# One step of a two-layer hybrid decoder: the order of TensorE's work inside a unit of the prompt's attention

## The reference

```
s[q, k] = q.k / 8 + c[q] - c[k]      causal; c: running sum of log forget values
o       = softmax(s) . v
```

## Time and profile before

| | |
|---|---|
| median of 3 runs | 1531.43 us (1527.56 to 1536.17) |
| the profiled execution's own time | 1532.03 us |
| its span | 1530.2 us |
| mean granted TensorE clock | 0.961 of full speed |
| busy share of the span: TensorE, VectorE, ScalarE, GpSimd | 93%, 33%, 32%, 39% |
| the loop over the units | from about 899.4 to 1040.3 us of the span |

### The profile page before, as it was taken

The page is one execution under the profiler, slowest core; times in us unless marked ns, Lnnn a source line. Parts: engine busy times, 40 slices in busy tenths (PEclk is TensorE's granted clock), DMA queues, the critical chain, the costliest instruction groups (busy, mean ns, idle before and its releaser), DMA issues.

```text
span 1530.2 us, 30086 instructions
## 1 busy us (share of the span) xinstructions
PE 1416.5 (93%) x11701; PEld 1293.3 (85%) x11701; DVE 503.3 (33%) x719; ACT 482.1 (32%) x622; POOL 601.4 (39%) x295
## 2 busy tenths in 40 slices
PE   7999899799999999996999969997969999999995
PEld 5999858689999999995899934446969999999994
DVE  2353853720000000147311179796540000000035
ACT  2331212353433421224211232324354334331123
POOL 2333301565555554364323230000654554554351
PEclk9999978999999999998999979899989999999998
DMA  5222201213323232221689998670213233232211
GB/s 215 83 77 86 74 27 40 78 30 113 99 72 114 94 113 90 95 74 33 215 279 319 328 203 309 214 247 14 83 42 97 84 95 96 82 117 95 94 39 56
DMA packets 88020, 180.30 MB, mean 118 GB/s; under 512 B 30025, under 2 KB 30042, under 8 KB 87442
## 3 DMA queue, kind: packets, MB, share of 16 engines
q1 hardware_dynamic: 87202, 175.46, 35.3%
q0 software_dynamic: 752, 3.92, 1.2%
HBM read 173.29 MB, written 6.05 MB: 117 GB/s over the span
## 4 chain that ended last, share of the span: by engine, by line
PE 75%; DVE 12%; issue 5%; ACT 2%; SPq 2%; DMA 2%; POOL 1%; DVEq 0%; ACTq 0%; POOLq 0%
PE ps L837 63%; DVE x L1342 2%; DVE pj L1729 2%; DVE rstd L1317 1%; SPq L331 1%; PE ps L1190 1%; PE ps L1189 1%; POOL wl L698 1%; DVE x L1331 1%; PE ps L1024 1%; DVE rstd L1339 1%; PE ps L1141 1%; PE ps L956 1%; PE ps L1219 1%; DVE x L1308 1%
## 5 line engine op out<-in xcount | busy, mean ns | idle before, releaser
L698 POOL TENSOR_TENSOR wl<-raw,wh 128x1024 fp32r<-128x1024 f32 (+1 forms) x180 | 460.7, 2559 | 801.0 <-ACT wh L385 801.0
L837 PE MATMUL ps<-xh,wh 128*128 128x260 f32 x2368 | 487.4, 287 | 57.0 <-POOL xl L763 36.2
L837 PE MATMUL ps<-xh,wl 128*128 128x260 f32 x2368 | 479.8, 284 | 0.0
L837 PE MATMUL ps<-xl,wh 128*128 128x260 f32 x2368 | 479.5, 284 | 0.0
L385 ACT ACTIVATE wh<-raw 128x1024 fp32r<-128x1024 f32 (+1 forms) x180 | 201.1, 1117 | 762.7 <-PE ps L837 756.9
L837 PEld LDWEIGHTS ps<-xh,wh 128*128 128x128 f32 x2368 | 367.9, 190 | 72.5 <-issue 41.9
L837 PEld LDWEIGHTS ps<-xh,wl 128*128 128x128 f32 x2368 | 368.1, 190 | 0.0
L837 PEld LDWEIGHTS ps<-xl,wh 128*128 128x128 f32 x2368 | 367.6, 190 | 0.0
L1383 DVE TENSOR_TENSOR hid_t<-ps,gate_t 128x520 f32<-128x520 f32 x44 | 30.8, 700 | 476.7 <-PE ps L837 476.7
L837 PE MATMUL ps<-hh,wh 128*128 128x260 f32 x704 | 142.3, 283 | 0.0
L837 PE MATMUL ps<-hh,wl 128*128 128x260 f32 x704 | 141.6, 282 | 0.0
(11 more groups left out here) (277 smaller groups left out, 1139.5 us busy)
## 6 DMA issues: line engine op xcount, KB each, us to landing
raw<-in_w_f_in SPq DMA_DIRECT2D x88, 512.0 KB, 3.5
pages<-in_cache_kt SPq DMA_DIRECT2D x128, 256.0 KB, 4.2
pages<-in_cache_v SPq DMA_DIRECT2D x128, 256.0 KB, 4.2
raw<-in_w_f_out SPq DMA_DIRECT2D x32, 704.0 KB, 4.0
raw<-in_w_ab_in SPq DMA_DIRECT2D x24, 512.0 KB, 3.6
raw<-in_w_cd_in SPq DMA_DIRECT2D x20, 512.0 KB, 4.3
raw<-in_w_ab_out SPq DMA_DIRECT2D x8, 512.0 KB, 3.6
raw<-in_w_cd_out SPq DMA_DIRECT2D x8, 512.0 KB, 5.4
```

The source lines that it names most:

```text
L698: nc.gpsimd.tensor_tensor(wl[:, j % SPLIT, 0:b * P], raw[:, j, 0:b * P], wh[:, j % SPLIT, 0:b * P].bitcast(F32), ALU.subtract).then_inc(w_ ...
L837: mm = nc.tensor.matmul(out[h], w[:, slot, block_at * P:block_at * P + P], rows[:, k, HT * h:HT * h + HT], start=start and a, stop=stop and z)
```

## The change

In TensorE's loop the value slot of unit u is issued ahead of the scores of unit u + 1 instead of behind them. Nothing else is changed: the same instructions with the same waits, on all engines.

```diff
             with pe.Fori(0, 2) as i:
                 scores(i, 0)
                 for u in range(16):
+                    value_slot(i, u)
                     if u < 15:
                         scores(i, u + 1)
-                    value_slot(i, u)
                     turned(i, u)
                     if u > 0:
                         outputs(i, u - 1)
```

## The result

The changed kernel takes 1542.92 us in the median of 12 runs (1537.82 to 1547.58), the kernel before 1534.62 in the median of 12 (1527.56 to 1539.44). The ratio is 1.0055, with a 95% interval of 1.0036 to 1.0075: slower by some 8.4 us, 5.5 to 11.5. The forecast of +6.7 us lies in that interval and 1542.9 lies in the stated range, at its upper edge, but I held no change (within 0.5%) for the likeliest, and the ratio lies beyond that bound. By how much is not sharp: the interval reaches down to 0.36%; a second measurement of the same kernel, further down, gave 1.0064 (1.0039 to 1.0089). Two runs of kernels further down, far from all others of their kernel (2772.53 us of all_but_u0_first, and 1787.27 us of warm_u0_first), are left out of every number.

The account below looks back on a forecast made before the run. The prediction took a closed chain between VectorE and TensorE, every four units, to bound the kernel. Its terms, 8 x 0.99 - 1.2 = +6.7 us, gave a median of 1538.1 us, range 1533 to 1543.

Parts of the forecast that it names:

- The closed chain: Every four units of the loop: VectorE's half 7.83 us, then TensorE's half 8.00 us, together 15.83 us a group.
- not slower: Rival: in the steady groups VectorE alone sets the pace, later scores still come in time; 1530.2 us, chance 0.09.
- The 16 us more of VectorE's waits: Sign in the loop: VectorE's waits for scores would rise by about 16 us from 15.3.
- Its price: Value slot(2) ahead of scores(3) lengthens TensorE's half by 0.99 us, eight times per execution: 7.9 us.
- the new neighbours: Some five new seams a group on TensorE's half, 2 us less or more in all; taken as nothing.
- Value slot(1) "nothing": In TensorE's half, slot(1) ahead of scores(2) delays maximum(2), but TensorE is last by 0.15 us: costs nothing.
- Value slots(3) and (0): In VectorE's half, TensorE's work of 6.7 us fits in 7.83 in both orders: costs nothing.
- The pages, -1.2 us: At slot(4) of the first iteration, an earlier load lands 2.4 us earlier and removes 1.2 us of wait.
- My rival with late pages: Slot(4)'s load lands where it did: 1.5 us more than the forecast, 1539.6 us, chance 0.13.
- The first units and the turn, none moves: Iteration start and turn: scores(0), slot(0), scores(1) precede transposes(0) in either order, so no time changes.
- The clock rival: One more drop of TensorE's clock, most likely ending the second iteration: 4.7 us more, 1542.8 us, chance 0.14.
- Drops in every group: Rival: each group's new TensorE wait lowers the clock, eight drops at 4.7 us: 38 us, 1576, chance 0.02.

Follow-up runs that it names:

- all_but_u0_first: The changed kernel without its slot(0): every value slot with u > 0 ahead of the scores; 1.0071 to the kernel before.
- warm_u0_first: The kernel before plus unread filler products in TensorE's waits, and slot(0) of each iteration ahead of scores(1); 0.9984 to the kernel before.
- The two kernels with short taps: Kernel before and changed kernel, each with two of four taps cut from 512 to 8 columns; 0.9971 and 0.9976 to the kernel before.
- u0_late: The kernel before with slot(0) of each iteration behind transposes(0), ahead of scores(2); 1.0013 to the kernel before.
- warm_before: The kernel before, its order kept, plus products that nobody reads in TensorE's waits; 1.0016 to the kernel before.
- slots03_first: The kernel before with only the value slots of u % 4 = 0 and 3 ahead of the scores; 1.0034 to the kernel before.
- after_two_taps: The changed kernel with two of each unit's four taps cut from 512 to 8 columns; 0.9976 to the kernel before.

## Why the prediction was right or wrong

**The closed chain: right.** VectorE's half stayed at 7.83 us, TensorE's grew, in each of eight groups, and the waits ahead of transposes(3) became 0.93 us (1.23 in the first group) and 1.82 at the end of the iterations. The two kernels with short taps show that nothing else in the group costs. One sign that I had named was wrong: a maximum(3) that follows scaling(2) without a wait was to mean "not slower". It came, and the kernel is slower, because the slot had already held back maximum(2) and VectorE's own work from there led to maximum(3). The 16 us more of VectorE's waits could not have come out either: VectorE does the same work, so in a loop that I took to be 7.9 us longer its waits can't grow by twice that.

**Its price: 0.85 instead of 0.99.** Forecast 7.9 us for eight groups, measured 6.8 (0.85 or 0.86 in the five stretches that lie wholly at the upper clock, taken for all eight). TensorE's half held the slot's 0.99 us, but the new neighbours that I had put at nothing gave back 0.14: scores(2), now followed by transposes(1), took 1.65 us instead of 1.74 (959.37 to 961.02), and transposes(1) with outputs(0), now followed by a slot, 0.68 instead of 0.73 (961.02 to 961.70).

**Value slot(1) "nothing": wrong.** The step compared when TensorE and VectorE would be ready for maximum(3) with slot(2) moved as well, found them 0.15 us apart, and gave the whole price to slot(2). Slot(1) alone costs 0.74 us a group, slot(2) alone 1.00. Two paths of nearly equal length led to maximum(3), so either slot is enough: undoing slot(2) would have gained some 0.1 us a group, and undoing slot(1) nothing.

**Value slots(3) and (0): nearly right,** 0.13 us a group by themselves.

**The pages, -1.2 us: wrong.** I took the end of the bounds in which the load lands as much earlier as it starts. With the 480 KB issued at 900 to 902 and the loads behind it, they landed some 20 us behind the loop's start in either order, and with that transfer out of the way they took 3 to 4 us: it held them. My rival with late pages is what happened, once with a wait of 0.73 us (second profile) and once hidden by a start at the lower clock.

**"The first units and the turn, none moves", and with it a clock term of nothing: the step that failed.** Counted in instructions the step is true, scores(0), slot(0) and scores(1) come ahead of transposes(0) in either order. But these units run at the lower clock, and the sum took it that this lasts as long as before. The changed kernel's mean clock is 0.0033 lower (0.9572 and 0.9571 in 20 runs together, against 0.9605), and u0_first, which moves nothing but slot(0) in the two first units, is 1.0022 slower, 3.4 us, at a clock 0.0034 lower. The groups' 6.8 us are 0.44%, just inside the bound; measured are 0.55%. The terms do not add up exactly: 6.8 + 3.4 = 10.2 us, for 8.4 measured, which is inside its interval (5.5 to 11.5). The miss of the bound is small against the noise; what is clear of it is that the clock fell.

The clock rival was right that TensorE's clock would take a part, and wrong about the place: it was looked for at the end of the second iteration, where the stretch still shows 1.00. Drops in every group did not occur; the steady group shows 1.00 with waits of 0.93 us in it. The rule of the Trainium skill that I set beside it (TensorE: Matmul & The Clock Gate, "A second HAM failure mode: psum-queue depth-cycling") does not describe this loop: waits for scaling of up to 1.23 us a group left the clock alone.

**Open.** Why slot(0) ahead of scores(1) goes with a longer lower clock is not shown, nor whether it is the only cause: all_but_u0_first and u0_late have low clocks too (0.9584, 0.9586), each with an idle stretch of its own in the profile. Nor is it shown that slot(0)'s place matters only where the start is at the lower clock: warm_u0_first costs no time over warm_before, but its clock fell just there at the second start, and its pages came earlier.

## What to carry to other kernels

When two engines take turns in a closed loop, work of the one is free while the other's half runs and costs nearly its full length (here 0.74 to 1.00 us of 0.99) once it stands ahead of what the other waits for; find every point where the second engine is released, not only the last, because two paths of nearly equal length hide each other's cost. And a maximum that starts without a wait does not show that TensorE no longer sets the pace: look one step further back. A transfer that lands late should be traced to what else is on the queues before an earlier issue is counted as a gain. Behind idle time of TensorE, a reordering that counts as neutral in instructions can still change how long the lower clock lasts: read the granted clock of many runs beside their times.

## What the runs showed of the hardware

- Mean clock and time go together from run to run: 0.001 of mean granted clock is about 1.2 us in 1533 (118 runs of before).
- Waits of TensorE for pages of 2.26 and 4.07 us were followed by the lower clock (slots03_first, warm_before). A wait of 1.57 us was followed by it in all_but_u0_first, for 17 us, and not in after_two_taps; waits of 0.93 to 1.23 us once a group were not.
- In u0_first the lower clock at the start of the first iteration lasted through 20.4 us in which TensorE was busy for 20.3; the changed kernel had 12.7 us in one profile and 8 in another.
- A transfer of 480 KB held four 256 KB loads of another queue, issued 2 to 4 us behind it, back until some 20 us behind the loop's start (10.8 to 11.9 us each in before); without it a load landed in 3.5 us, and issued 0.3 us ahead of it four landed in 4.1 to 6.8 (warm_u0_first).
- The order outputs, slot, scores, transposes has seams 0.18 us a group shorter than the order before (15.34 against 15.52 us with the taps cut).
